# The MLP's up projection split at 512 + 128 token columns instead of 320 + 320, in a two-layer streaming encoder on one Trainium2 core

## The chip, the core and the metric

One NeuronCore of a Trainium2 chip runs the whole program. The metric is device time in microseconds, and less is better. The engines that matter here are TensorE (PE, with its weight loads shown apart as PEld), ScalarE (ACT), VectorE (DVE), GpSimd (POOL) and the queue that issues the transfers (SP). Matmul results land in PSUM, which has 8 banks of 128 partitions x 512 fp32 columns.

## The reference

640 tokens go through two layers: 512 prompt tokens of one stream and 8 running streams of 16 sample tokens each. Each layer has a mixer (retention heads and a short convolution) and an MLP. Cut to what the change touches:

```python
D_MODEL, D_FF = 1024, 4096
def hybrid_layer(x, ...):
    n = rms_norm(x, ln1_w)
    proj = n @ w_in                     # 1024 -> 3584
    ...                                 # retention, short convolution
    x = x + jnp.concatenate([ret_out, conv_out], axis=-1) @ w_out
    h2 = rms_norm(x, ln2_w)
    x = x + jnp.square(jax.nn.relu(h2 @ w_up)) @ w_down
    return x, r_new, new_buf
```

## The kernel before

Every large product is made at nearly fp32 precision from rounded parts: each operand is held as a high part (`w_hi`, `norm_hi`, `inner_hi`, type float32r) and a low part (`w_lo`, `norm_lo`, `inner_lo`), and a product is three matmuls, hi x hi, hi x lo and lo x hi, all added up in one PSUM bank. The rest (scores, states, transposes) runs on plain fp32.

The MLP is done in blocks of 512 of the 4096 hidden features (`NBLK` = 8). `up_block(b)` on TensorE makes the block's hidden features with the features on the partitions: 4 tiles of 128 features (`ft`) times 2 halves of the 640 token columns, so `UPS` = 8 groups, numbered j = half * 4 + ft. A group is made by `features_product` (L479): for 8 pieces k of the contraction and 3 pairs of parts, one matmul with a 128x128 piece of the weights as the stationary operand and `HALF` = 320 token columns of `norm_hi` or `norm_lo` as the moving one. That is 24 matmuls a group, 192 a block, and 3072 over 8 blocks and 2 layers; each loads its own weights. `features_product` also makes the mixer's C, H and B products (L479, 1152 matmuls). `down_block(d)` goes through `tokens_product` (L469): 10 groups of 12 matmuls with 512 moving columns. The order is up 0, then up 1, down 0, up 2, down 1 and so on.

A group takes the next of six PSUM banks (`mlp_bank`). ACT applies relu from the bank into one of four `relu` buffers (L880), DVE squares it in place (L1345), ACT rounds it into `inner_hi` (L871), and DVE subtracts for `inner_lo` (L1338). Beside that ACT rounds each next weight unit into `w_hi` (L685) and DVE makes `w_lo` (L1046). `add_into_x` (L1313) adds the down products into `x`.

The tokens are normalised before the MLP tile by tile (5 tiles of 128; tiles 0 to 3 are the prompt, tile 4 the sample). For tile t, in this order: the output product's last group `("O", 1, t)`, the addition into `x` (DVE L1313), the square and its sum (ACT L703), the root (POOL L926, L929), `xn` (DVE L1065), and two turns `("n2", t, c)`, each four transposes on TensorE (L519), which ACT reads into `norm_hi` (L732) and DVE into `norm_lo` (L1089). `TURN_AFTER` puts tile t-1's turns behind group `("O", 1, t)`; those of tile 4 come by hand after the first up block's group j = 1. DVE's list has, for each tile t, the addition, `normalise` of tile t, and only then the low parts of tile t-1; ACT's has the square of tile t and then the high parts of tile t-1. In `up_block(0)` the first group of each half waits for the tiles that its columns need: 320 columns reach into tile 2, so half 0 waits for tile 2's turns, and half 1 for those of tile 4 (`NT - 1`).

Of the kernel before, what the change touches and what calls it, by code (L numbers as in the profile page):

```python
# [17 lines left out]
DEPTH, D, TOK, SEQ, NB, NS = 2, 1024, 640, 512, 8, 16  # L18
P = 128
NT = TOK // P  # L20
# [2 lines left out]
H, HD, RW, CW = 4, 128, 512, 512  # L23
FT = CW // P
HALF = TOK // 2
NBLK = 4 * D // 512
UPAD = SEQ + 2 + NB * (NS + 2)
LN_EPS, GN_EPS = 1e-6, 1e-5
# [18 lines left out]
PER_BLOCK = UPS + DOWNS  # L47
PER_LAYER = MIX + NBLK * PER_BLOCK
CHUNKS = MIX_CHUNKS + 2 * NBLK
WARMING = 7  # L50
# [3 lines left out]
MIX_VECTOR = [n for n, g in enumerate(GROUPS) if g[0] not in SCALAR_READS]  # L54
SCALAR_PER_LAYER = len(MIX_SCALAR) + NBLK * UPS
VECTOR_PER_LAYER = len(MIX_VECTOR) + NBLK * DOWNS

# [14 lines left out]
TURN = {x: n for n, x in enumerate(TURNS)}  # L72
# [57 lines left out]
def program(nc, x_p, x_s, state_ret, state_conv, norm_rows, ln2_w, w_in, conv_w, ret_w, w_out, w_up, w_down,  # L130
            consts, y_p, y_s, new_ret_p, new_conv_p, new_ret_s, new_conv_s):
    f32, f32r = mybir.dt.float32, mybir.dt.float32r
    ALU, ACT = mybir.AluOpType, mybir.ActivationFunctionType
# [3 lines left out]
    with ctx:  # L137
# [3 lines left out]
        def place(name, shape, dt, offset=None):  # L141

            size = 4 * int(np.prod(shape[1:]))
            if offset is None:
                offset = at[0]
                at[0] += (size + 31) // 32 * 32
            return nc.alloc_sbuf_tensor_at(name, shape, dt, offset=offset)
# [16 lines left out]
        inner_hi = place("inner_hi", [P, KT, TOK], f32r, inner_at)  # L164
        inner_lo = place("inner_lo", [P, KT, TOK], f32r, inner_at + 2 * quarter)
# [13 lines left out]
        vo_at = region(FT * UPAD * 4 + 32)  # L179
        v = place("v", [P, NT, RW], f32, vo_at)  # L180
        o = place("o", [P, NT, RW], f32, vo_at)
        u = place("u", [P, FT, UPAD], f32, vo_at)
        relu = place("relu", [P, 4, HALF], f32, vo_at)


        temp_at = region(10 * KB)
# [44 lines left out]
        mlp_bank = mix_bank + small_bank  # L231
# [52 lines left out]
        hidden_hi = Signal("hidden_hi", NBLK * UPS)  # L284
# [160 lines left out]
        def _(pe):  # L445
            three = ((0, 0), (0, 1), (1, 0))
            norms, inners, ws = (norm_hi, norm_lo), (inner_hi, inner_lo), (w_hi, w_lo)
# [22 lines left out]
                                       start=(n == 0 and m == 0), stop=(n == len(ks) - 1 and m == 2))  # L470
                return mm

            def features_product(out, ft, half, par, before=None):

                for k in range(KT):
                    if before:
                        before(k)
                    for m, (a, b) in enumerate(three):
                        mm = pe.matmul(out, ws[a][:, par, k // 4, k % 4, ft * P:(ft + 1) * P],  # L479
                                       norms[b][:, k, half * HALF:(half + 1) * HALF],  # L480
                                       start=(k == 0 and m == 0), stop=(k == KT - 1 and m == 2))
                return mm

# [86 lines left out]
            with pe.Fori(0, DEPTH) as layer:  # L570
                for n, g in enumerate(GROUPS):
                    stage, chunk = g[0], max(c for c in range(MIX_CHUNKS) if STAGE_START[c] <= n)
                    par, out = chunk % 2, mix_bank[n % 3]
# [6 lines left out]
                    if stage == "K":  # L580

                        last = TURN["n1", g[1], 1]
# [19 lines left out]
                    if stage in "KVQGO":  # L602
                        tile = {"O": g[-1], "G": g[1]}.get(stage, ORDER[g[1]] if stage in "KVQ" else None)
                        act = inners if stage == "O" else norms
                        mm = tokens_product(out[:], tile, act, range(KT),
                                            lambda b, k: ws[b][:, par, k // 4, k % 4], weights_there)
                    else:
                        mm = features_product(out[:, 0:HALF], g[1], g[2], par, weights_there)
                    mm.then_inc(group_done.sem, 1)
# [5 lines left out]
                def up_block(b):  # L615
                    first = isinstance(b, int) and b == 0
                    par, start = parity_up(first), 0 if first else UPS
                    for j in range(UPS):
                        half, ft = divmod(j, FT)
                        if first and j < 3:  # L620
                            pe.wait_ge(vector_read.sem, vector_read.at(layer, len(MIX_VECTOR) - 2 + j))
                        if not first and j < 6:
                            pe.wait_ge(vector_read.sem, vector_read.at(
                                layer, b * DOWNS + (len(MIX_VECTOR) - DOWNS - 5 + j)))
                        if not (first and j < 6):
                            pe.wait_ge(scalar_read.sem, scalar_read.at(layer, b * UPS + (len(MIX_SCALAR) - 5 + j)))
                        if first and ft == 0:
                            last = TURN["n2", 2 if half == 0 else NT - 1, 1]
                            pe.wait_ge(turn_read.sem, turn_read.at(layer, last + 1))
                            pe.wait_ge(turn_lo.sem, turn_lo.at(layer, split_turns_to(last)))  # L630

                        def weights_there(k, j=j):
                            if j == 0 and k % 4 == 0:
                                wait_unit(layer, up_chunk(b), k // 4)

                        mm = features_product(mlp_bank[(start + j) % 6][:, 0:HALF], ft, half, par, weights_there)
                        mm.then_inc(group_done.sem, 1)
                        if first and j == 1:
                            turn(layer, ("n2", NT - 1, 0))
                            turn(layer, ("n2", NT - 1, 1))  # L640
# [39 lines left out]
        def _(act):  # L680
# [69 lines left out]
            with act.Fori(0, DEPTH) as layer:  # L750
# [16 lines left out]
                for p in range(NT):  # L767
                    n = GROUP["V", p]
# [14 lines left out]
                for t in range(NT):  # L783
                    n = GROUP["G", t]
# [21 lines left out]
                for ft in range(FT):  # L806
                    for half in range(2):
                        n = GROUP["C", ft, half]
                        act.wait_ge(group_done.sem, group_done.at(layer, n + 1))
                        src = mix_bank[n % 3]  # L810
                        if half == 0:
                            ins = nc.scalar.activation(u[:, ft, 2:2 + HALF], src[:, 0:HALF], ACT.Copy)
                        else:
                            rest = SEQ - HALF
                            nc.scalar.activation(u[:, ft, 2 + HALF:2 + SEQ], src[:, 0:rest], ACT.Copy)
# [27 lines left out]
                for ft in range(FT):  # L843
                    for half in range(2):
                        act.wait_ge(vector_read.sem, vector_read.at(
                            layer, MIX_VECTOR.index(GROUP["B", ft, half]) + 1))
                        cols = slice(half * HALF, (half + 1) * HALF)
# [17 lines left out]
                def up_block(b, buf, chunk, par, before):  # L865
                    split_chunk(layer, chunk, par, before)

                    def hi_part(j):
                        half, ft = divmod(j, FT)
                        act.wait_ge(squared.sem, squared.at(layer, b * UPS + (j + 1)))  # L870
                        nc.scalar.activation(inner_hi[:, buf * FT + ft, half * HALF:(half + 1) * HALF],  # L871
                                             relu[:, j % 4], ACT.Copy).then_inc(hidden_hi.sem, 1)

                    first = isinstance(b, int) and b == 0
                    for j in range(UPS):
                        act.wait_ge(group_done.sem, group_done.at(layer, up_group(b, j + 1)))
                        if not (first and j < 4):
                            act.wait_ge(hidden_lo.sem, hidden_lo.at(layer, b * UPS + (j - 3)))
                        slot = (0 if first else UPS) + j
                        nc.scalar.activation(relu[:, j % 4], mlp_bank[slot % 6][:, 0:HALF], ACT.Relu  # L880
                                             ).then_inc(scalar_read.sem, 1)
                        if j >= 1:
                            hi_part(j - 1)
                    hi_part(UPS - 1)
# [152 lines left out]
        def _(dve):  # L1037
# [155 lines left out]
            with dve.Fori(0, DEPTH) as layer:  # L1193
# [61 lines left out]
                for ft in range(FT):  # L1255
                    for half in range(2):
                        n = GROUP["H", ft, half]
# [30 lines left out]
                for ft in range(FT):  # L1288
# [9 lines left out]
                    for half in range(2):  # L1298
                        n = GROUP["B", ft, half]
# [15 lines left out]
                for t in range(NT):  # L1315
                    n = GROUP["O", 0, t]
# [3 lines left out]
                for t in range(NT):  # L1320
                    n = GROUP["O", 1, t]
# [11 lines left out]
                def up_block(b, buf, chunk, par):  # L1333
                    def lo_part(j):
                        half, ft = divmod(j, FT)
                        cols = slice(half * HALF, (half + 1) * HALF)
                        dve.wait_ge(hidden_hi.sem, hidden_hi.at(layer, b * UPS + (j + 1)))
                        nc.vector.tensor_tensor(inner_lo[:, buf * FT + ft, cols], relu[:, j % 4],  # L1338
                                                f(inner_hi[:, buf * FT + ft, cols]), ALU.subtract
                                                ).then_inc(hidden_lo.sem, 1)  # L1340

                    for j in range(UPS):
                        dve.wait_ge(scalar_read.sem, scalar_read.at(
                            layer, b * UPS + (len(MIX_SCALAR) + j + 1)))
                        nc.vector.tensor_tensor(relu[:, j % 4], relu[:, j % 4], relu[:, j % 4], ALU.mult  # L1345
                                                ).then_inc(squared.sem, 1)
                        if j >= 1:
                            lo_part(j - 1)
                        if j in (0, 1):
                            split_unit(layer, chunk, j, par)  # L1350
                    lo_part(UPS - 1)
# [77 lines left out]
```

## Time and profile before

| | |
|---|---|
| median of 3 runs | 1497.02 us (1496.27 to 1497.89) |
| the profiled execution's span, first to last instruction | 1495.1 us |
| TensorE busy in it | 1480.4 us (99%), 8326 matmuls |
| TensorE weight loads | 1336.0 us (89%), 8326 |
| DVE, ACT, POOL busy | 651.8, 393.8, 126.3 us |
| mean granted TensorE clock | 0.998 |

The profile comes from one execution; its span leaves out what lies before the first and after the last instruction. A matmul's duration runs from its start to the modelled arrival of its results, so neighbouring matmuls overlap in the rows, and the time that one costs in a stream is the spacing of two starts, not its duration. The same holds for weight loads.

### The profile page before, as it was taken

To read this page: it belongs to the slowest core of one execution; us is meant where nothing else is said; L and a number is where in the kernel's file an instruction comes from. 1 tells how busy PE (TensorE), PEld (TensorE's weight loads), DVE (VectorE), ACT (ScalarE), POOL (GpSimd) and SP (SyncE) were. 2 spreads that over 40 slices of the span, in tenths; PEclk is the share of its full clock that TensorE was granted. 3 is DMA by queue.
4 is the path that set the end of the run, shared out by engine and by line. 5 is a ranking of instruction groups with operands and counts; after the bars stand their busy time and mean duration, and the time that the engine had idled before them with its cause. 6 is when DMAs were issued, how large, how long until landed. Compare 5 with 4: busy or idle time off the path is not lost.

```text
span 1495.1 us, 21805 instructions
## 1 busy us (share of the span) xinstructions
PE 1480.4 (99%) x8326; PEld 1336.0 (89%) x8326; DVE 651.8 (44%) x970; ACT 393.8 (26%) x579; POOL 126.3 (8%) x153
## 2 busy tenths in 40 slices
PE   7999999999999999999999999999999999999998
PEld 6888999899989989989888889988999899889886
DVE  5346435355334334334362562444543433433433
ACT  5212222233123222222142203213422223223121
POOL 2343100000000000000033330000000000000000
PEclk9999999999999999999999999999999999999999
DMA  7323112122212213213042231221131221221301
GB/s 257 128 85 114 64 57 84 59 85 82 89 57 93 75 56 108 74 57 120 1 133 80 85 114 64 78 94 57 62 109 57 84 85 56 90 93 56 106 8 71
DMA packets 74643, 124.27 MB, mean 83 GB/s; under 512 B 3332, under 2 KB 20868, under 8 KB 74568
## 3 DMA queue, kind: packets, MB, share of 16 engines
q1 hardware_dynamic: 74424, 123.18, 24.9%
q8 instruction: 50, 0.82, 0.2%
q14 instruction: 25, 0.20, 0.0%
q10 hardware_dynamic: 144, 0.07, 0.0%
HBM read 115.83 MB, written 7.41 MB: 82 GB/s over the span
## 4 chain that ended last, share of the span: by engine, by line
PE 99%; DVE 0%; ACT 0%; DMA 0%; issue 0%; POOL 0%; DVEq 0%; POOLq 0%; ACTq 0%
PE bank L469 51%; PE bank L479 41%; PE bank L519 2%; PE bank L557 1%; PE bank L564 1%; PE bank L538 1%; PE bank L542 0%; PE bank L547 0%; PE bank L550 0%; DMA x<-in_x_sample 0%; PE bank L555 0%; DVE norm_lo L1089 0%; DVE w_lo L1054 0%; DVE xn L1065 0%; ACT L691 0%
## 5 line engine op out<-in xcount | busy, mean ns | idle before, releaser
L479 PE MATMUL bank<-norm_hi,w_hi 128*128 128x320 f32 x1408 | 436.1, 310 | 0.0
L479 PE MATMUL bank<-norm_hi,w_lo 128*128 128x320 f32 x1408 | 435.3, 309 | 0.0
L479 PE MATMUL bank<-norm_lo,w_hi 128*128 128x320 f32 x1408 | 435.3, 309 | 0.0
L469 PE MATMUL bank<-w_hi,inner_hi 128*128 128x512 f32 x800 | 312.1, 390 | 0.0
L469 PE MATMUL bank<-w_lo,inner_hi 128*128 128x512 f32 x800 | 311.6, 389 | 0.0
L469 PE MATMUL bank<-w_hi,inner_lo 128*128 128x512 f32 x800 | 311.5, 389 | 0.0
L685 ACT ACTIVATE w_hi<-w_raw 128x2048 fp32r<-128x2048 f32 x96 | 178.7, 1907 | 350.1 <-PE bank L469 322.4
L479 PEld LDWEIGHTS bank<-norm_hi,w_hi 128*128 128x128 f32 x1408 | 264.4, 188 | 0.6
L479 PEld LDWEIGHTS bank<-norm_lo,w_hi 128*128 128x128 f32 x1408 | 264.4, 188 | 0.5
L479 PEld LDWEIGHTS bank<-norm_hi,w_lo 128*128 128x128 f32 x1408 | 264.4, 188 | 0.0
L1313 DVE TENSOR_TENSOR x<-x,bank 128x512 f32<-128x512 f32 x180 | 123.6, 687 | 293.9 <-PE bank L469 293.9
L1046 DVE TENSOR_TENSOR w_lo<-w_raw,w_hi 128x2048 fp32r<-128x2048 f32 (+1 forms) x100 | 219.7, 2201 | 5.5 <-ACT w_hi L685 5.5
L1345 DVE TENSOR_TENSOR relu<-relu 128x320 f32<-128x320 f32 x128 | 63.0, 492 | 265.6 <-ACT relu L880 265.6
L469 PEld LDWEIGHTS bank<-w_hi,inner_lo 128*128 128x128 f32 x800 | 150.2, 188 | 31.3
L469 PEld LDWEIGHTS bank<-w_lo,inner_hi 128*128 128x128 f32 x800 | 150.2, 188 | 30.4
L469 PEld LDWEIGHTS bank<-w_hi,inner_hi 128*128 128x128 f32 x800 | 150.2, 188 | 30.4
L469 PE MATMUL bank<-w_hi,norm_hi 128*128 128x512 f32 x320 | 129.1, 404 | 2.5 <-DVE w_lo L1054 2.5
L880 ACT ACTIVATE relu<-bank 128x320 f32<-128x320 f32 x128 | 55.6, 436 | 282.5 <-PE bank L479 282.5
L469 PE MATMUL bank<-w_hi,norm_lo 128*128 128x512 f32 x320 | 125.7, 393 | 0.0
L469 PE MATMUL bank<-w_lo,norm_hi 128*128 128x512 f32 x320 | 125.5, 392 | 0.0
L926 POOL TENSOR_SCALAR var<-sums 128x1 f32<-128x1 f32 x25 | 4.8, 191 | 1196.7 <-ACT xn L703 1191.0
L469 PEld LDWEIGHTS bank<-w_hi,norm_hi 128*128 128x128 f32 x320 | 60.5, 189 | 15.2 <-ACT w_hi L691 2.9
(104 smaller groups left out, 918.1 us busy)
## 6 DMA issues: line engine op xcount, KB each, us to landing
w_raw<-in_w_mlp_up SPq DMA_DIRECT2D x32, 1024.0 KB, 5.4
w_raw<-in_w_mlp_down SPq DMA_DIRECT2D x32, 1024.0 KB, 5.0
w_raw<-in_w_in SPq DMA_DIRECT2D x28, 1024.0 KB, 5.1
w_raw<-in_w_out SPq DMA_DIRECT2D x8, 1024.0 KB, 5.0
past_state<-in_state_ret SPq DMA_DIRECT2D x8, 512.0 KB, 4.1
out_ret_s<-past_state SPq DMA_DIRECT2D x8, 512.0 KB, 4.9
x<-in_x_prompt SPq DMA_DIRECT2D x4, 512.0 KB, 12.4
norm_row<-in_norm_rows SPq DMA_DIRECT2D x3, 512.0 KB, 5.6
```

What stands on the lines that cost most here:

```text
L469: mm = pe.matmul(out, act[a][:, k, tile * P:(tile + 1) * P], w_of(b, n), start=(n == 0 and m == 0), stop=(n == len(ks) - 1 and m == 2))
L479: mm = pe.matmul(out, ws[a][:, par, k // 4, k % 4, ft * P:(ft + 1) * P], norms[b][:, k, half * HALF:(half + 1) * HALF], start=(k == 0 and ...
L519: mm = pe.transpose(out[:, i * P:(i + 1) * P], src[i], identity)
L538: mm = pe.matmul(out[:, h * P:(h + 1) * P], kT[:, ORDER[p], h], qT, start=True, stop=True)
L557: mm = pe.matmul(out[:, 0:HD], q_spread[:, b], past_state[h % 2][:, b], start=False, stop=(b == NB - 1))
L564: mm = pe.matmul(out[:], k_rot[:, SAMPLE, h * HD:(h + 1) * HD], v_spread[:, 4 * c:4 * c + 4], start=True, stop=True)
L685: nc.scalar.activation(w_hi[:, par, half], w_raw[:, half], ACT.Copy).then_inc(w_hi_ready.sem, 1)
L880: nc.scalar.activation(relu[:, j % 4], mlp_bank[slot % 6][:, 0:HALF], ACT.Relu).then_inc(scalar_read.sem, 1)
L926: nc.gpsimd.tensor_scalar(tmp, src, scale, eps, ALU.mult, ALU.add).then_inc(eps_step.sem, 1)
L1046: ins = nc.vector.tensor_tensor(w_lo[:, par, half, ks], w_raw[:, half, ks], f(w_hi[:, par, half, ks]), ALU.subtract)
L1313: nc.vector.tensor_tensor(xx, xx, src[:], ALU.add).then_inc(vector_read.sem, 1)
L1345: nc.vector.tensor_tensor(relu[:, j % 4], relu[:, j % 4], relu[:, j % 4], ALU.mult).then_inc(squared.sem, 1)
```

## The change

The two token parts of an up group become 0:512 (the prompt) and 512:640 (the sample). The number of groups, of matmuls and of weight loads stays the same, and so does the number of columns over both parts. `relu` buffers grow from 320 to 512 columns. The first group of the first up block now waits for the turns of tile 3, since 512 columns reach to the end of it. The mixer's products keep 320 + 320.

```diff
+PARTS_UP = [slice(0, SEQ), slice(SEQ, TOK)]
...
-        relu = place("relu", [P, 4, HALF], f32, vo_at)
+        relu = place("relu", [P, 4, SEQ], f32, vo_at)
...
-            def features_product(out, ft, half, par, before=None):
-
+            def features_product(out, ft, half, par, before=None, cols=None):
+
+                cols = cols or slice(half * HALF, (half + 1) * HALF)
...
-                                       norms[b][:, k, half * HALF:(half + 1) * HALF],
+                                       norms[b][:, k, cols],
...
                         if first and ft == 0:
-                            last = TURN["n2", 2 if half == 0 else NT - 1, 1]
+                            last = TURN["n2", 3 if half == 0 else NT - 1, 1]
                             pe.wait_ge(turn_read.sem, turn_read.at(layer, last + 1))
                             pe.wait_ge(turn_lo.sem, turn_lo.at(layer, split_turns_to(last)))
...
-                        mm = features_product(mlp_bank[(start + j) % 6][:, 0:HALF], ft, half, par, weights_there)
+                        cols = PARTS_UP[half]
+                        mm = features_product(mlp_bank[(start + j) % 6][:, 0:cols.stop - cols.start], ft, half, par,
+                                              weights_there, cols)
...
-                        nc.scalar.activation(inner_hi[:, buf * FT + ft, half * HALF:(half + 1) * HALF],
-                                             relu[:, j % 4], ACT.Copy).then_inc(hidden_hi.sem, 1)
+                        cols = PARTS_UP[half]
+                        nc.scalar.activation(inner_hi[:, buf * FT + ft, cols], relu[:, j % 4, 0:cols.stop - cols.start],
+                                             ACT.Copy).then_inc(hidden_hi.sem, 1)
...
-                        nc.scalar.activation(relu[:, j % 4], mlp_bank[slot % 6][:, 0:HALF], ACT.Relu
+                        n = PARTS_UP[j // FT].stop - PARTS_UP[j // FT].start
+                        nc.scalar.activation(relu[:, j % 4, 0:n], mlp_bank[slot % 6][:, 0:n], ACT.Relu
                                              ).then_inc(scalar_read.sem, 1)
...
-                        cols = slice(half * HALF, (half + 1) * HALF)
+                        cols = PARTS_UP[half]
...
-                        nc.vector.tensor_tensor(relu[:, j % 4], relu[:, j % 4], relu[:, j % 4], ALU.mult
+                        cols = PARTS_UP[j // FT]
+                        r = relu[:, j % 4, 0:cols.stop - cols.start]
+                        nc.vector.tensor_tensor(r, r, r, ALU.mult
                                                 ).then_inc(squared.sem, 1)
```

## Rows read from the trace of the kernel before

**Rows 1.** The page's first two parts: span, and the busy time of each engine.
```profile
span 1495.1 us, 21805 instructions
PE 1480.4 (99%) x8326; PEld 1336.0 (89%) x8326; DVE 651.8 (44%) x970; ACT 393.8 (26%) x579; POOL 126.3 (8%) x153
```

**Rows 2.** The chain that ended last, in order of time: start us, us, what.
```profile
557.14 28.16 PE bank L479 x192
585.29 27.23 PE bank L469 x120
```

**Rows 3.** The same view, stretches of plain fp32 matmuls of 128 and of 512 columns.
```profile
99.60 1.79 PE bank L557 x16
101.39 1.72 PE bank L564 x4
```

**Rows 4.** Timeline, start us, us: four loads for 16-column transposes.
```profile
166.54 0.32 PEld L511 LDWEIGHTS bank<-const,conv_rows 16*128 16x128 f32 x4 [0.17 <-issue]
```

**Rows 5.** Timeline: two float32r weight loads after TensorE had waited.
```profile
756.93 1.28 DVE L1089 TENSOR_TENSOR norm_lo<-bank,norm_hi 128x512 fp32r<-128x512 f32 x2
...
758.27 0.19 PEld L469 LDWEIGHTS bank<-w_hi,norm_hi 128*128 128x128 f32 x1 [0.34 <-DVE norm_lo L1089]
...
758.38 0.19 PEld L469 LDWEIGHTS bank<-w_lo,norm_hi 128*128 128x128 f32 x1
```

**Rows 6.** Groups by line and shape: out<-in xcount, busy us, mean ns, idle before.
```profile
L479 PEld LDWEIGHTS bank<-norm_hi,w_hi 128*128 128x128 f32 x1408 | 264.4, 188 | 0.6
...
L557 PEld LDWEIGHTS bank<-past_state,q_spread 128*128 128x128 f32 x128 | 14.9, 192 | 0.0
```

**Rows 7.** The same view: the evacuations of 320 columns, and those of 128.
```profile
L1345 DVE TENSOR_TENSOR relu<-relu 128x320 f32<-128x320 f32 x128 | 63.0, 492 | 265.6 <-ACT relu L880 265.6
...
L880 ACT ACTIVATE relu<-bank 128x320 f32<-128x320 f32 x128 | 55.6, 436 | 282.5 <-PE bank L479 282.5
...
L770 ACT ACTIVATE v<-bank 128x512 f32<-128x512 f32 x10 | 6.0, 598 | 38.9 <-PE bank L469 38.8
...
L1270 DVE TENSOR_TENSOR u<-u,bank 128x128 f32<-128x128 f32 x8 | 2.2, 281 | 0.0
L816 ACT ACTIVATE u<-bank 128x128 f32<-128x128 f32 x8 | 2.2, 273 | 0.0
```

**Rows 8.** Timeline before the first up block, layer 0, and its last row in layer 1.
```profile
305.53 1.03 PE L519 MATMUL bank<-const,xn 128*128 128x128 f32 x8
305.73 0.69 DVE L1313 TENSOR_TENSOR x<-x,bank 128x512 f32<-128x512 f32 x1 [0.93 <-PE bank L469]
...
307.51 1.06 ACT L732 ACTIVATE norm_hi<-bank 128x512 fp32r<-128x512 f32 x2
...
308.64 1.28 DVE L1065 SCALAR_TENSOR_TENSOR xn<-x,rstd,norm_row 128x1024 f32<-128x1024 f32 x1 [2.22 <-POOL rstd L929]
309.85 1.28 DVE L1089 TENSOR_TENSOR norm_lo<-bank,norm_hi 128x512 fp32r<-128x512 f32 x2
...
1047.64 1.28 DVE L1089 TENSOR_TENSOR norm_lo<-bank,norm_hi 128x512 fp32r<-128x512 f32 x2
```

**Rows 9.** The chain in order of time, where the first up blocks begin.
```profile
306.57 7.04 PE bank L479 x48
...
1044.37 7.04 PE bank L479 x48
```

**Rows 10.** Timeline of TensorE in the mixer's first group, after it had waited.
```profile
12.64 0.47 PE L469 MATMUL bank<-w_hi,norm_hi 128*128 128x512 f32 x1 [2.10 <-DVE w_lo L1054]
...
14.49 0.63 PE L469 MATMUL bank<-w_hi,norm_hi 128*128 128x512 f32 x1
14.92 0.63 PE L469 MATMUL bank<-w_lo,norm_hi 128*128 128x512 f32 x1
```

**Rows 11.** The stretch around it, by the view of stretches; the first line names the columns.
```profile
core 0: us, PE busy (x) PEld busy (x) DVE busy (x) ACT busy (x) POOL busy (x), PEclk, DMA share, GB/s
...
12.60:18.00 5.40, 5.36 (x21) 4.34 (x22) 4.36 (x7) 5.37 (x10) 1.64 (x3) 0.68 1.02 407
```

More of the change, by code:

```diff
@@ L1335, in lo_part @@
                         half, ft = divmod(j, FT)
-                        cols = slice(half * HALF, (half + 1) * HALF)
+                        cols = PARTS_UP[half]
                         dve.wait_ge(hidden_hi.sem, hidden_hi.at(layer, b * UPS + (j + 1)))
-                        nc.vector.tensor_tensor(inner_lo[:, buf * FT + ft, cols], relu[:, j % 4],
+                        nc.vector.tensor_tensor(inner_lo[:, buf * FT + ft, cols], relu[:, j % 4, 0:cols.stop - cols.start],
                                                 f(inner_hi[:, buf * FT + ft, cols]), ALU.subtract
```

## The prediction

> **What bounds the kernel now.** I read the busy times first: TensorE is busy for 1480.4 of 1495.1 us, and no other engine for more than 651.8 [rows 1]. That share alone doesn't say what a matmul costs, because neighbouring matmuls overlap in the rows. So I went to the chain that ended last, in order of time, where a stretch of matmuls and its count give the spacing of two starts. An up block takes 28.16 us for 192 matmuls of 320 columns, 146.7 ns each; a down block 27.23 us for 120 of 512 columns, 226.9 ns each [rows 2]. The reader should see that the two lie on one line: (226.9 - 146.7) / 192 columns = 0.418 ns a column, which is the higher clock of 2.4 GHz, and 146.7 - 320 x 0.418 = 13 ns for each matmul, whatever its width. Then the evacuations: relu on ACT and the square on DVE take 0.436 and 0.492 us a group, and those engines sat 282.5 and 265.6 us waiting for TensorE and for each other [rows 7]. TensorE's stream is the bound, and only what changes this stream, or makes it wait, moves the time.
>
> **The change, part by part.**
>
> *The stream itself.* 3072 matmuls of 320 columns (8 blocks x 8 groups x 24, twice) become 1536 of 512 and 1536 of 128. Columns and instructions stay the same in number. On the line above, a narrow one would take 13 + 128 x 0.418 = 66.8 ns, a pair 226.9 + 66.8 = 293.7 instead of 2 x 146.7 = 293.4, and the sum would be 1536 x 0.3 ns = 0.5 us. So even by the line there is nothing to win.
>
> But the line only holds while the weight load hides behind the matmul before it. Each matmul loads its own 128x128 weights. A load's row lasts 188 ns [rows 6], longer than the 146.7 ns between two loads in an up block, so loads overlap in the rows and this duration is not their price. The price shows where nothing covers the load: after a wait TensorE starts the load of a float32r tile at 758.27 and the load for the next matmul at 758.38 [rows 5]. The second can only go once the first set of weights has been taken over, so a load by itself costs 0.11 us (0.105 to 0.115 with the rounding). Three other waits in the trace show the same distance. 320 columns stream for 133 ns and hide that; 128 columns stream for 53 ns and do not. So in a stream of narrow matmuls I expect one per load, some 110 ns.
>
> The trace of before has no float32r matmul under 320 columns, so I bound it. The nearest rows are plain fp32 ones of 128 columns with the same size of load (192 ns a row against 188 [rows 6]): 16 in 1.79 us, 112 ns each [rows 3]. They fit both readings, since they also stream longer. The ends: 66.8 ns if the load were hidden; 110 + 13 = 123 ns if the fixed 13 ns comes on top of the load. I take 112 ns, the row with the same width and size of load, next to the measured 110. A pair is then 226.9 + 112 = 338.9 ns, 45.5 more than before, and 1536 x 45.5 ns = 69.9 us. Ends of this term: at 105 ns 38.6 x 1536 = 59.3 us, at 123 ns 56.6 x 1536 = 86.9 us.
>
> The Trainium skill, "TensorE: Matmul & The Clock Gate", section "LDWEIGHTS (loading the stationary operand)", gives a load as its columns over 1.2 GHz, an estimate of 107 ns for 128. By that the trace agrees within its rounding, and the rule speaks against this change. The same page's section "Back-to-back issue gap" gives 81 ns for a matmul of 128 columns with its load in a stream; by it a pair would be 307.9 ns and this term, as an estimate, 1536 x 14.5 = 22 us. No run here shows 81.
>
> *The new wait.* Half 0 of the first up block now waits for the turns of tile 3. Before, it began at 306.57, straight behind those transposes [rows 9]. What it must now wait for is at the end of a chain: the addition of the last output group on DVE (305.73), the square, the root on GpSimd, tile 4's `xn` (308.64), and only then, because DVE works in order, the low parts of tile 3, which end at 309.85 + 1.28 = 311.13 [rows 8]. The high parts on ACT are done by 308.57 [rows 8], so DVE is what ends last. From the end of such a low part to TensorE's load took 758.27 - 758.21 = 0.06 us, and the uncovered load 0.11 [rows 5]: the stream starts at 311.30, 4.73 us late. In layer 1 the low parts end at 1048.92, start 1049.09 against 1044.37, 4.72 us [rows 8, 9]. Both: 9.4 us. Nothing covers this, since every later group is queued behind the waiting one on TensorE, tile 4's transposes too. ACT and DVE wait for nothing more than before. The lower bound is the ACT end, 308.57 + 0.17, a stall of 2.2 us each (4.3 us), if DVE's part were not needed, which the code excludes.
>
> *The clock after that wait.* After an idle time of 2.10 us near the start [rows 10], matmuls of 512 columns came 0.43 us apart, the lower level of 1.2 GHz, and the stretch of 5.40 us was granted 0.68 on average: 5.40 x 0.32 = 1.7 us lost [rows 11]. A stop of 4.7 us is longer, so I take 1.7 us for each layer, 3.4 us; the ends are 0 and twice as much.
>
> *The evacuations.* A block's relus take 4 x (0.598 + 0.273) = 3.5 us, before 8 x 0.436 = 3.5. A narrow group lasts 24 x 112 ns = 2.7 us, against 0.27 to 0.28 us for each of its ACT and DVE steps; a wide one 5.4 us against about 0.6 to 0.7 [rows 7]. Six banks and four relu buffers are turned over later than they are free. In the first block tile 4's turns are needed by j = 4 only, two wide groups after they are made. The block as a whole gets longer (32.5 us), so weights rounded for the next stage and their transfers get more time. All of this I put at nothing; its cover is TensorE's own stream, and if it failed it would show as TensorE waiting for ACT or DVE.
>
> *Sum.* 1495.1 + 69.9 + 9.4 + 3.4 = 1577.8 us of span. The median of the runs lies 1.9 us above the profiled span (1497.02), so I forecast 1579.7 us.
>
> **The rivals.**
>
> *Loads overlap and are hidden.* The 188 ns rows at a spacing of 146.7 ns speak for loads that run into each other, and four loads for transposes of 16 columns take 0.32 us together, so at most 80 ns each [rows 4]: there is a faster way to load. Against it: transposes load differently from float32r tiles, whose uncovered load was 110 ns. A narrow matmul then takes 66.8 ns and only the wait remains: 1497.0 + 0.5 + 9.4 + 3.4 = 1510.3 us. With 81 ns in place of 66.8 it would be 1532, by the page named above.
>
> *Narrow float32r matmuls lose their fast rate.* Nothing under 320 columns runs at the single-pass rate in this trace. If a narrow one costs what an fp32 product of 128 columns costs, two records of 112 ns [rows 3], a pair takes 450.9 ns: 1536 x 157.5 = 241.9 us, 1751.8 us in all. A narrow stream at the 1.2 GHz level with a load that slows alike would come out about there as well. For it there is only the absence of rows; against it that the load explains the nearest row.
>
> *The clock falls in the narrow groups.* The array streams 53 of every 112 ns for 10.7 us a block. If that counts as too little work, the next wide groups start at the lower level. At the 1.7 us of [rows 11], 16 narrow stretches cost 27 us: 1606.9 us. Against it: through all transposes and small products of the mixer the mean clock stays at 0.998; but those stream more densely.
>
> *The other side: not slower.* If the 13 ns is itself the part of the load that sticks out, and a narrow matmul runs at 53.3 ns plus the 3 ns that the plain fp32 ones of 512 columns have over their own streaming (1.72 / 4 = 430 ns against 2 x 213.3 [rows 3]), a pair takes 283.5 ns, 9.9 less, and 1536 x 9.9 = 15.2 us is won against 12.8 of wait and clock: 1494.6 us. It decides from a narrow spacing of 58 ns down, half of what the uncovered load took. The Trainium skill's page named above, section "Back-to-back issue gap", has 128 / 2.4 + 2.5, an estimate of 55.8 ns, for a matmul by itself; by it the result would be about 1494 us. The rows of uncovered loads speak against it.
>
> **How the numbers follow.** Forecast 0.72; clock falls in the narrow groups 0.08; slow narrow rate 0.10; loads hidden 0.07; not slower 0.03. The range takes in the first two: below 1497.0 + 59.3 + 9.4 + 0 = 1565.7, above the 1606.9 of the clock case, or 1497.0 + 86.9 + 9.4 + 6.8 = 1600.1 for the forecast's own upper end; I round to 1565 and 1610. 0.20 is left out. A measurement of this kernel can tell about 0.2%, 3 us, from no change. Only the last rival can give faster (0.02) or the same (0.01), all others are slower (0.97).
>
> **What would show it.** In the profile after: an up block of some 32.5 us in the chain, 96 matmuls at 227 ns and 96 at 110 to 124 ns; load rows of 188 ns starting 110 ns apart in the narrow groups; TensorE at L479 waiting twice for DVE's `norm_lo`, 4 to 5 us each, with a granted clock under 1 behind it; down blocks still at 27.2 us. The forecast is wrong if narrow loads start closer than 100 ns or further than 125 ns apart, if the down blocks get longer (the clock), or if ACT or DVE show up as what TensorE waits for inside the blocks.

## The result: 1581.83 us, 5.6% slower

| | before | after |
|---|---|---|
| median | 1497.45 us (1496.27 to 1498.14, 4 runs) | 1581.83 us (1581.24 to 1583.06, 4 runs) |
| ratio | | 1.0564, 95% interval 1.0549 to 1.0579 |
| profiled span | 1495.1 us | 1580.9 us |
| TensorE busy | 1480.4 us | 1556.4 us |

The page after, against [rows 1]: the same number of instructions on each engine, TensorE 76 us busier, DVE and ACT by less than 3 us, GpSimd not at all.

```profile
span 1580.9 us, 21805 instructions
PE 1556.4 (98%) x8326; PEld 1348.8 (85%) x8326; DVE 653.4 (41%) x970; ACT 396.5 (25%) x579; POOL 126.3 (8%) x153
```

The chain that ended last in the changed kernel, in order of time (start us, us, what), over the first up block and two stages behind it; against [rows 2] and [rows 9]:

```profile
312.58 13.99 PE bank L481 x48
...
381.56 27.31 PE bank L470 x120
408.87 32.43 PE bank L481 x192
...
1093.39 12.77 PE bank L481 x48
```

An up block went from 28.16 to 32.43 us, a down block from 27.23 to 27.31. The first two groups of a layer's first up block are a case of their own: 48 matmuls of 512 columns would take 48 x 226.9 ns = 10.9 us, and took 13.99 and 12.77.

The timeline of the changed kernel where wide groups end and narrow ones begin, weight loads first (start us, us):

```profile
609.24 0.19 PEld L481 LDWEIGHTS bank<-norm_hi,w_lo 128*128 128x128 f32 x1
609.46 0.19 PEld L481 LDWEIGHTS bank<-norm_hi,w_hi 128*128 128x128 f32 x1
609.69 0.19 PEld L481 LDWEIGHTS bank<-norm_lo,w_hi 128*128 128x128 f32 x1
609.80 0.19 PEld L481 LDWEIGHTS bank<-norm_hi,w_lo 128*128 128x128 f32 x1
609.91 0.19 PEld L481 LDWEIGHTS bank<-norm_hi,w_hi 128*128 128x128 f32 x1
```

and the matmuls themselves a little later, ten of them in a row, first and last:

```profile
609.97 0.27 PE L481 MATMUL bank<-norm_hi,w_hi 128*128 128x128 f32 x1
...
610.97 0.28 PE L481 MATMUL bank<-norm_hi,w_hi 128*128 128x128 f32 x1
```

Nine distances in 1.00 us: 111 ns. The load's own row is as long as before, 0.19 us, and does not tell its price. What changes is its distance to the next one: 0.23 us under a wide matmul and 0.11 under a narrow one.

The very first matmul of the narrow groups looks different. Its own load stood beside a wide matmul, and the next matmul's row starts only 0.05 us after it; from then on the distance is 0.11 (first three narrow matmuls, timeline):

```profile
609.69 0.22 PE L481 MATMUL bank<-norm_hi,w_hi 128*128 128x128 f32 x1
609.74 0.28 PE L481 MATMUL bank<-norm_lo,w_hi 128*128 128x128 f32 x1
609.86 0.27 PE L481 MATMUL bank<-norm_hi,w_lo 128*128 128x128 f32 x1
```

Four other blocks, in both layers, show the same: 0.05 or 0.06 us, and the same shorter row of 0.22.

The start of the first up block in layer 0 (timeline; in brackets the idle time and what ended it), against [rows 8]:

```profile
306.75 1.04 PE L521 MATMUL bank<-const,xn 128*128 128x128 f32 x8
...
311.06 1.28 DVE L1095 TENSOR_TENSOR norm_lo<-bank,norm_hi 128x512 fp32r<-128x512 f32 x2
312.58 0.77 PE L481 MATMUL bank<-norm_hi,w_hi 128*128 128x512 f32 x1 [4.80 <-DVE norm_lo L1095]
313.15 0.63 PE L481 MATMUL bank<-norm_lo,w_hi 128*128 128x512 f32 x1
313.57 0.63 PE L481 MATMUL bank<-norm_hi,w_lo 128*128 128x512 f32 x1
...
318.66 0.39 PE L481 MATMUL bank<-norm_hi,w_lo 128*128 128x512 f32 x1
318.89 0.40 PE L481 MATMUL bank<-norm_hi,w_hi 128*128 128x512 f32 x1
```

TensorE stands for 4.80 us and then works at 0.43 us a matmul, the 1.2 GHz level. It is back at 0.23 after 6.1 us. The view of stretches has the granted clock (the column before the last two) at 0.50 in between:

```profile
315.00:317.00 2.00, 2.00 (x7) 1.52 (x6) 0.00 (x0) 0.00 (x0) 0.00 (x0) 0.50 0.00 0
```

**Where 85.8 us of span went.** Each pair of a wide and a narrow group cost more: 16 up blocks x 4.27 us = 68.3 us, and 14 down blocks that follow a narrow group x 0.08 = 1.1 us (the load of the first wide matmul stands beside a narrow one and is not covered either: that matmul's row starts at 441.13 and the next at 441.43, 0.30 us apart where the others are 0.23). The stops are 2 x 4.8 = 9.6 us. The slow start behind them is 13.99 - 10.9 and 12.77 - 10.9, together 5.0 us. Nearly all of it is the lower clock; with the clock at its upper level a start behind a stop still took 11.13 us (last experiment below), so 0.2 us of each is something else, and the clock's own part is 2.9 and 1.6, together 4.5 us. That makes 84.0. Of the other 1.8 us, 1.2 are at hand before the change's code is reached: the transposes that started at 305.53 [rows 8] start at 306.75. They lie at the start of the program, where the mixer's first 12 matmuls began 0.4 us later and took 5.41 us where they had taken 4.57. The last 0.6 us were not followed up.

### The profile page after: what moved, and what is told of

It reads as the page before. It is cut to its first block, busy times and chain, and to the rows that moved or that the text cites. A ratio compares the mean times of both kernels' runs of the same rounds, so it can differ in the third digit from the quotient of the medians.

```text
span 1580.9 us, 21805 instructions
## 1 busy us (share of the span) xinstructions
PE 1556.4 (98%) x8326; PEld 1348.8 (85%) x8326; DVE 653.4 (41%) x970; ACT 396.5 (25%) x579; POOL 126.3 (8%) x153
## 4 chain that ended last, share of the span: by engine, by line
PE 98%; issue 1%; DVE 1%; DMA 0%; ACT 0%; POOL 0%; DVEq 0%; POOLq 0%; ACTq 0%
PE bank L470 48%; PE bank L481 44%; PE bank L521 2%; PE bank L559 1%; PE bank L566 1%; PE bank L540 1%; PE bank L544 0%; PE bank L549 0%; PE bank L552 0%; DMA x<-in_x_sample 0%; DVE norm_lo L1095 0%; DVE x L1319 0%; PE bank L557 0%; POOL rstd L935 0%; ACT xn L707 0%
## 5 line engine op out<-in xcount | busy, mean ns | idle before, releaser
L481 PE MATMUL bank<-norm_hi,w_hi 128*128 128x512 f32 (+2 forms) x1408 | 460.9, 327 | 9.6 <-DVE norm_lo L1095 9.6
L481 PE MATMUL bank<-norm_lo,w_hi 128*128 128x512 f32 (+2 forms) x1408 | 460.5, 327 | 0.0
L481 PE MATMUL bank<-norm_hi,w_lo 128*128 128x512 f32 (+2 forms) x1408 | 460.3, 327 | 0.0
L481 PEld LDWEIGHTS bank<-norm_lo,w_hi 128*128 128x128 f32 x1408 | 267.6, 190 | 20.7
L481 PEld LDWEIGHTS bank<-norm_hi,w_lo 128*128 128x128 f32 x1408 | 267.6, 190 | 20.5
L1353 DVE TENSOR_TENSOR relu<-relu 128x512 f32<-128x512 f32 (+1 forms) x128 | 62.9, 491 | 310.3 <-ACT relu L886 310.3
L886 ACT ACTIVATE relu<-bank 128x512 f32<-128x512 f32 (+1 forms) x128 | 55.7, 437 | 339.2 <-PE bank L481 339.2
```

The costliest lines, as they stand in the source:

```text
L886: nc.scalar.activation(relu[:, j % 4, 0:n], mlp_bank[slot % 6][:, 0:n], ACT.Relu).then_inc(scalar_read.sem, 1)
L1353: nc.vector.tensor_tensor(r, r, r, ALU.mult).then_inc(squared.sem, 1)
```

## Experiments

Each has its theories' numbers as written before it ran. "Kernel before" was run beside each, at 1497.3 or 1497.4 us.

### Is it the load or the width? 384 + 256

```diff
-PARTS_UP = [slice(0, SEQ), slice(SEQ, TOK)]
+PARTS_UP = [slice(0, 384), slice(384, TOK)]
...
-                            last = TURN["n2", 3 if half == 0 else NT - 1, 1]
+                            last = TURN["n2", 2 if half == 0 else NT - 1, 1]
```

> The up projection takes 384 + 256 columns; half 0 then ends inside tile 2 and waits for tile 2's turns, as in the kernel before. Theory L (load): a matmul of N columns is spaced max(13 + 0.418 N, 111.6) ns, the second being the uncovered load of its own weights. 256 columns take 120.0 ns and cover the load, 384 take 173.5, a pair 293.5 against 293.4 before: up block 28.2 us, total within 2 us of 1497. Theory W (width): float32r matmuls of few columns stream at half rate, 0.833 ns a column plus 5, and 128 happened to give 111.6 for that reason. If 256 is still wide, 1497 as well; if it counts as narrow, 218 ns, pair 392, up block 37.6 us, total about 1648.

1497.48 us, ratio 1.0002 (0.9992 to 1.0012): the same as before. The chain has an up block at

```profile
390.30 28.17 PE bank L481 x192
```

A group of 256 columns spaces its matmuls 119.9 ns, one of 384 173.4. An uneven split by itself costs nothing. Both theories allowed that, so this run rules out only that 256 columns count as few.

### 448 + 192

```diff
-PARTS_UP = [slice(0, SEQ), slice(SEQ, TOK)]
+PARTS_UP = [slice(0, 448), slice(448, TOK)]
```

> 448 + 192 columns; half 0 reaches into tile 3 and keeps the new wait. Theory L: 192 columns would stream in 93.3 ns by the line, less than the load, so they are spaced 111.6 ns, the same as 128 columns; 448 take 200.3. Pair 311.9, up block 29.9 us, total 1497.4 + 1536 x 18.5 ns = 28.4, plus the wait and clock of the first block as in the changed kernel (about 15): 1541. Theory W (half rate under some width): 192 columns take 165 ns, pair 365, up block 35.1 us, total 1622.

1544.36 us (two runs), ratio 1.0313 (1.0293 to 1.0334). The timeline of its narrow groups, first and last row of 95 in a row (one of the 96 records is missing), and the chain:

```profile
422.09 0.28 PE L481 MATMUL bank<-norm_lo,w_hi 128*128 128x192 f32 x1
...
432.58 0.28 PE L481 MATMUL bank<-norm_hi,w_lo 128*128 128x192 f32 x1
```
```profile
402.71 30.15 PE bank L481 x192
```

10.49 us over 94 distances is 111.6 ns: 192 moving columns cost what 128 cost. Half rate would have been 165. The moving width doesn't set the spacing here; theory W falls. The block is 0.25 us longer than expected because the 448-column matmuls take (30.15 - 96 x 0.1116) / 96 = 202.5 ns, 2 more than the line gives. Why was not followed up.

### Half of the weight columns in the narrow groups

```diff
-                        mm = pe.matmul(out, ws[a][:, par, k // 4, k % 4, ft * P:(ft + 1) * P],
+                        few = cols.stop - cols.start == P and (k, m) not in ((0, 0), (KT - 1, 2))
+                        n = P // 2 if few else P
+                        mm = pe.matmul(out[0:n], ws[a][:, par, k // 4, k % 4, ft * P:ft * P + n],
```

> The changed kernel, but in each narrow group 22 of the 24 matmuls load only 64 of the 128 weight columns (the other 64 features of the sample tokens get only the first and the last of the 24 products, so this part of the result is left out). The moving width stays 128. Theory L: a load of 64 columns by itself is about half of 111 ns, 58, and hides behind... the 66.8 ns of the line; narrow groups go from 2.68 to 22 x 66.8 + 2 x 111.6 = 1.69 us, up block 28.5 us, total 1581.8 - 64 x 0.99 = 1518. Theory W (moving width decides): nothing changes, 1582 and 2.68 us a narrow group.

1509.32 us (two runs), ratio 1.0079 (1.0059 to 1.0099). The moving width is still 128; the load is half as long, and most of the loss is gone. What is left, 12 us, is the wait and the slow start behind it, some 15 us in this run, less what up blocks of 27.87 us in place of 28.16 give back. Timeline of the loads, where two full ones stand between short ones, then an up block in the chain:

```profile
422.27 0.19 PEld L483 LDWEIGHTS bank<-norm_hi,w_lo 128*128 128x128 f32 x1
422.38 0.19 PEld L483 LDWEIGHTS bank<-norm_hi,w_hi 128*128 128x128 f32 x1
422.50 0.14 PEld L483 LDWEIGHTS bank<-norm_lo,w_hi 128*64 128x64 f32 x1
422.56 0.14 PEld L483 LDWEIGHTS bank<-norm_hi,w_lo 128*64 128x64 f32 x1
```
```profile
397.82 27.87 PE bank L483 x192
```

0.11 us behind a full load, 0.06 behind a short one. The edit also halves the features that a matmul writes, `out[0:n]`, so by itself it leaves a rival: that the 111 ns are the narrow matmul's own cost with 128 output features. The rows of the changed kernel above speak against it: the first narrow matmul has all 128 features and its load beside a wide one, and it is short, a row of 0.22 us with the next 0.05 us behind. Here the same first matmul and the half one behind it are equally long:

```profile
419.42 0.22 PE L483 MATMUL bank<-norm_hi,w_hi 128*128 128x128 f32 x1
419.47 0.22 PE L483 MATMUL bank<-norm_lo,w_hi 128*64 128x128 f32 x1
```

So the load of the weights is the cause. I had expected 66.8 ns and 1518 us: the fixed 13 ns, read off the wide matmuls, do not hold for 128 columns.

### A quarter of the weight columns

The same edit with `n = P // 4`.

> As the run with 64 weight columns in the narrow groups, now 32 (three quarters of the features get only two of the 24 products, left out on purpose). With 128 weight columns a narrow matmul was spaced 111 ns, with 64 it was 60 ns. Theory A (at 64 columns the load still sets the spacing): with 32 it falls again, to the streaming of 128 moving columns plus a few ns at most, 55 ns. Theory B (at 64 columns the streaming of the moving operand already set it, 53.3 + 6.7): it stays at 60 ns, and the total at 1509.

1509.7 us (two runs), ratio 1.0083 (1.0063 to 1.0103), and still 0.06 us apart:

```profile
422.26 0.11 PEld L483 LDWEIGHTS bank<-norm_hi,w_hi 128*32 128x32 f32 x1
422.32 0.11 PEld L483 LDWEIGHTS bank<-norm_lo,w_hi 128*32 128x32 f32 x1
```

Theory B. 60 ns is what 128 moving columns need once no load sticks out: 53.3 for the streaming at 2.4 GHz and 6.7 more. So the narrow matmul of the change pays 111 - 60 = 51 ns for its load.

### Are the 13 ns of a wide matmul part of the load?

The edit of the half load, made in the kernel before with its 320 + 320.

> The kernel before (320 + 320), with 22 of 24 matmuls of each up group loading only 64 weight columns (half of the features get only two of the 24 products, left out on purpose to shorten the load alone). Asks what the 13 ns are that each float32r matmul has over its streaming. Theory F (fixed, no part of the load): spacing stays 146.7 ns, up block 28.16 us, 1497. Theory P (a part of the load that sticks out and shrinks with it): 13 ns fall to about 6, up block 28.16 - 176 x 0.0065 = 27.0 us, total about 1479.

1496.93 us, ratio 0.9996 (0.9987 to 1.0006); an up block in the chain:

```profile
391.85 28.16 PE bank L481 x192
```

No part of them is the load: theory F for 320 columns. What they are stays open, as does why 128 columns have only 6.7.

### Can the wide matmul's slack pay for the narrow one's load? Interleaved

```diff
+            def both_parts(wide, narrow, ft, par, before):
+
+                for k in range(KT):
+                    before(k)
+                    for m, (a, b) in enumerate(three):
+                        for out, cols in zip((wide, narrow), PARTS_UP):
+                            mm = pe.matmul(out[:, 0:cols.stop - cols.start],
+                                           ws[a][:, par, k // 4, k % 4, ft * P:(ft + 1) * P], norms[b][:, k, cols],
+                                           start=(k == 0 and m == 0), stop=(k == KT - 1 and m == 2))
...
```

In blocks 1 to 7 `up_block` calls this in place of two single groups, and ACT and DVE take the groups in the new order. The first block stays as in the change.

> The changed kernel, but in blocks 1 to 7 the wide and the narrow matmul of each weight tile are issued in turn (wide, narrow, wide, narrow, two banks at once) instead of 96 wide and then 96 narrow ones. Theory L1 (a load starts only when the weights before it are taken over, one set ahead): the narrow one's load hides behind the wide one, but the next wide one's load starts with the narrow matmul and takes its 111 ns; pair 227 + 111 = 338 ns, up block 32.4 us, total 1582 as before. Rival L2 (loads can run further ahead, so the wide matmul's slack of 100 ns can be used for two loads): pair 294 ns, up block 28.2 us, total 1497.4 + 15 + 2 x 4.3 = 1521.

1584.28 us, ratio 1.0582 (1.0564 to 1.0599). The timeline of the loads (two merged in a row) and an up block in the chain:

```profile
410.11 0.30 PEld L499 LDWEIGHTS bank<-norm_hi,w_lo 128*128 128x128 f32 x2
410.45 0.30 PEld L499 LDWEIGHTS bank<-norm_hi,w_hi 128*128 128x128 f32 x2
```
```profile
347.70 32.67 PE bank L499 x192
```

A pair takes 0.34 us = 0.23 + 0.11, no less than when kept apart. A wide matmul hides one load, not two: the narrow one's load is hidden, and the next wide one's is not, though 100 ns of the wide matmul are left over. L1 holds; in this stream one set of weights is made ready ahead.

### The wait by itself

```diff
-                            last = TURN["n2", 2 if half == 0 else NT - 1, 1]
+                            last = TURN["n2", 3 if half == 0 else NT - 1, 1]
```

in the kernel before, nothing else.

> The kernel before with its 320 + 320 columns and one edit: the first up block's half 0 waits for tile 3's turns instead of tile 2's. This is the wait of the change by itself. Theory S (the wait and the clock behind it are a term of their own): TensorE stands 4.8 us twice, and the clock falls behind it; in the changed kernel the two first group pairs took 13.99 and 12.77 us instead of 10.9, so 3.1 and 1.9 us more. Total 1497.4 + 9.6 + about 5 = 1512. Rival: the wait is hidden or given back later (ACT and DVE catch up, the next stages begin with more in hand), and the total is within 3 us of 1497.

1511.26 us, ratio 1.0095 (1.0078 to 1.0112): 13.9 us, not hidden and not given back. Its first 48 matmuls of 320 columns took 9.69 us in the chain where [rows 9] has 7.04, so the clock falls behind the stop here too (the granted clock of the whole run is 0.994 against 0.998):

```profile
311.01 9.69 PE bank L479 x48
```

### The change without the wait

The first up block keeps 320 + 320 and tile 2's wait, blocks 1 to 7 are changed (`parts_up(b)` in place of `PARTS_UP`).

> The changed kernel, but the first up block of each layer keeps 320 + 320 and tile 2's wait; blocks 1 to 7 take 512 + 128. Theory S: the wait and its clock loss go (9.6 + 5.0 us), and with them two blocks' worth of narrow groups (2 x 4.3): 1581.8 - 14.6 - 8.6 = 1558.6. Rival (the wait costs nothing in the end): only the 8.6 us go, 1573.

1558.11 us, ratio 1.0409 (1.0391 to 1.0426). The 23.7 us below the changed kernel are the 8.6 us of two blocks and 15.1 of wait and clock. Wait and narrow groups are two terms that add up to within about a microsecond: the wait with its clock costs 13.9 alone, and gives 15.1 when taken away.

### What the wait is made of

On DVE, tile 3's low parts before tile 4's normalisation:

```diff
+                    if t == NT - 1:
+                        for c in range(2):
+                            read_turn_lo(layer, ("n2", t - 1, c))
                     normalise(layer, NT, t, t, 32)
-                    if t >= 1:
+                    if 1 <= t < NT - 1:
```

> The changed kernel with DVE's order turned at one place: the low parts of tile 3 come before the normalisation of tile 4. Theory O (the wait is as long as it is because of DVE's order): DVE's low parts then follow ACT's high parts directly, ending 1.6 us earlier; TensorE stands 3.2 instead of 4.8 us, twice, so 3.2 us less, 1578.6, or a few us less if the shorter stop also spares the clock (down to 1574). Rival (ACT or the transposes set it): no change, 1581.8.

1576.68 us, ratio 1.053 (1.0513 to 1.0548), 5.2 us less than the change. The stop is 3.08 us, and the clock still falls, but one microsecond after the start (1.4 in layer 1), and the 48 matmuls take 12.76 us:

```profile
309.68 0.47 PE L481 MATMUL bank<-norm_hi,w_hi 128*128 128x512 f32 x1 [3.08 <-DVE norm_lo L1095]
...
310.75 0.63 PE L481 MATMUL bank<-norm_lo,w_hi 128*128 128x512 f32 x1
311.18 0.63 PE L481 MATMUL bank<-norm_hi,w_lo 128*128 128x512 f32 x1
```

Then also on ACT, the high parts before the wait for tile 4's addition and its square:

```diff
                 for t in range(NT):
+                    if t == NT - 1:
+                        for c in range(2):
+                            read_turn(layer, ("n2", t - 1, c))
                     act.wait_ge(vector_read.sem, vector_read.at(
...
-                    if t >= 1:
+                    if 1 <= t < NT - 1:
```

> The changed kernel with both orders turned: on ACT the high parts of tile 3 come before the square of tile 4, on DVE the low parts before tile 4's normalisation (the run before turned DVE's alone: stop 3.1 us, clock still fell, 1576.7). Expected: high parts end 1.3 us earlier, so TensorE stands about 1.8 us, twice, 2.6 us less: 1574. If a stop of 1.8 us leaves the clock at its upper level, the 1.9 us lost in each layer are saved as well: 1570.4. Rival: the stop does not get shorter, because what ends last is something else (DVE's addition, the transposes): 1576.7.

1571.48 us, ratio 1.0495 (1.0477 to 1.0512). The stop is 1.76 us, twice, and the matmuls behind it stay at 0.23, with a granted clock of 1.00; the chain has the 48 at 11.13 us, 0.2 above 10.9:

```profile
308.62 0.47 PE L481 MATMUL bank<-norm_hi,w_hi 128*128 128x512 f32 x1 [1.76 <-DVE norm_lo L1098]
308.92 0.40 PE L481 MATMUL bank<-norm_lo,w_hi 128*128 128x512 f32 x1
...
310.07 0.39 PE L481 MATMUL bank<-norm_hi,w_hi 128*128 128x512 f32 x1
```
```profile
308.62 11.13 PE bank L481 x48
```

So two thirds of the stop were the order of work on DVE and ACT, as the chain of the prediction had it, and the clock loss goes with it. None of the kernels beats the one before: the two splits with at least 256 columns in each part (320 + 320 and 384 + 256) measured the same, with no loss and nothing to win.

## Why the prediction was right, step by step

- *TensorE's stream is the bound.* Right. Neither ACT nor DVE is what TensorE waits for in any block; the only new wait is the one at `norm_lo`.
- *The line, 13 ns + 0.418 N, so nothing to win.* Right from 256 to 512 columns (119.9, 146.7, 173.4, 226.8 ns; only 448 columns lie 2 ns above it), and 384 + 256 measured the same as 320 + 320. The prediction's "whatever its width" is wrong at 128: without the load in the way 128 columns take 60 ns, not the 66.8 that it gives. That touched the rival of hidden loads only; with 60 it would come to 1497.4 - 10 + 14.6 = 1502 instead of 1510.
- *The load sets the narrow spacing, 112 ns, 69.9 us.* Right: 111 ns, and 68.3 + 1.1 = 69.4 us. The row that carried it, two loads 0.11 us apart after a wait [rows 5], gave the price within its rounding, 0.105 to 0.115; the duration of 188 ns said nothing. The figure of 112 came from plain fp32 matmuls, which, as the prediction says, fit both readings; that it lies within 1 ns of the result is in part luck.
- *The new wait, 4.73 and 4.72 us.* Right: 4.80 twice, ended by DVE's low parts. The run of the wait alone and the two turned orders show that it is the chain described. From the low part's end to the matmul's row took 312.58 - 312.34 = 0.24 us, a little more than the 0.17 taken.
- *The clock behind the wait, 1.7 us a layer.* The mechanism was right, the term was mis-sized: 3.1 and 1.9 us, 5.0 together instead of 3.4, inside the ends of 0 and 6.8 (4.5 of it with a lower clock, by the 11.13 us of the last run). The slow stretch of [rows 10, 11] was taken as the size of any such stretch; this one lasted 6.1 us in layer 0 and 3.5 in layer 1.
- *The evacuations at nothing.* Right: DVE's and ACT's times on the profile's page moved by less than 3 us, none of it on the chain.
- *Sum* 1579.7 against 1581.83. That it came so near is in part errors that cancel. In the span, 3.1 us were missing: the stream was put 0.5 too high, the stops 0.2 too low, the clock term 1.6 too low, and 1.8 were no term at all. The step from span to median was put at 1.9, and is 0.9 here, because the profiled run was the slowest of the four.

Of the rivals, slow narrow matmuls fell with the 111 ns, where they had 224, and a milder form of them with 448 + 192; hidden loads fell with the same 111 ns and the half load, the other side with the 60 ns that remain even without a load (the point it had to reach was 58 with the load). The clock in the narrow groups did not fall. "The down blocks get longer" was a sign of being wrong, and by its letter it came true, 27.31 for 27.23 us; but the view of stretches has the down block behind the narrow groups at a granted clock of 1.00, and the extra 0.08 is at its first load:

```profile
441.30:468.60 27.30, 27.30 (x121) 22.56 (x121) 11.19 (x14) 4.48 (x5) 0.00 (x0) 1.00 0.23 78
```

The forecast of an up block of 32.5 us was met at 32.43.

The Trainium skill, "TensorE: Matmul & The Clock Gate", section "LDWEIGHTS (loading the stationary operand)", gives the load as its columns over 1.2 GHz, an estimate of 107 ns for 128; the spacing of 111 ns lies 4 ns above it, and agrees with the load as what bounds a narrow float32r matmul. The 81 ns for a matmul of 128 columns with its load, in its section "Back-to-back issue gap", don't hold for this type: no float32r stream here with full loads came under 111, and the measurement decides. (Its 55.8 ns for a matmul by itself would have made 1493.4 us by the prediction's own terms, not 1494.)

## What to carry to other kernels

Where every matmul loads its own weights, as in the float32r streams here from 128 to 512 columns, a matmul costs the larger of two times: its streaming with its fixed part, or its load, which took 111 ns. Splitting columns unevenly adds the shortfall of every matmul that drops under the load's price, and the surplus of its wide neighbour doesn't pay for it, not even interleaved. Read the price of a load from the distance of two loads after a wait, where nothing hides it, not from the length of a row. When a cut moves past a tile's edge, follow the work that produces that tile to its end on each in-order engine: the wait cost 14 to 15 us here, and about a third of that was the slower work behind it.

## What had not been expected of the hardware

- The fixed part of a float32r matmul is not one number: 13 ns at 256 to 512 moving columns, 6.7 at 128 (60.0 ns with 64 or 32 weight columns). It doesn't depend on the load: 320 columns stay at 146.7 ns with 64 weight columns.
- The lower clock after a stop came at once, or 1.0 and 1.4 us late, and the slow start cost 1.9 to 3.1 us a time after stops of 3.1 and 4.8 us; after stops of 1.8 us it did not come, twice. Near the start of the program it came after one of 2.1 us [rows 10].
- One float32r matmul hides one load and no more: a pair of 512 and 128 columns in turn took 0.34 us, though the wide one has time left over.
